# One trunk layer: RWKV products dealt to 64x64 tiles, gate projections spread over the four rounds, another order at the feed-forward entry

## The reference, cut to what matters

```
x = x + 0.5 * SwiGLU(RMSNorm(x))                 # feed-forward 1, D_FF = 2816
h = RMSNorm(x); P = h @ w_in                      # attention q,k,v | RWKV r,k,v,lora | 2 x 1024 gate columns
A = dilated window attention(P)                   # three groups
R = RWKV-7 time mixing(P)                         # 8 heads of 64, matrix state 64x64
x = x + w_out(sigmoid(gA) * (A @ w_branch_attn) + sigmoid(gR) * (R @ w_branch_rwkv))
x = x + 0.5 * SwiGLU(RMSNorm(x))                 # feed-forward 2

def step(S, r, w, k, v, kk, a):                   # RWKV-7, for each token in turn
    sk = S @ kk
    S = S * w - outer(sk, kk * a) + outer(v, k)
    return S, S @ r
```

## Time and profile before

| | before |
|---|---|
| median of three runs | 1737.68 us (1736.03 to 1738.81) |
| own time of the profiled execution | 1736.48 us |
| its span | 1734.6 us |
| PE busy | 1681.9 us, 97% of the span |
| DVE, ACT, POOL busy | 953.0, 737.8, 710.2 us (55, 43, 41%) |
| chain that ended last | PE 85%, DVE 9%, ACT 2% |
| fills and units, L396 | three passes, 1232 matmuls each |
| rounds 1, 2, 3 of RWKV begin | 552.11, 640.20, 729.22 us |
| next stage begins on PE | 803.67 us |

### The profile page before, as it was taken

The page is one execution under the profiler, slowest core; times in us unless marked ns, Lnnn a source line. Parts: engine busy times, 40 slices in busy tenths (PEclk is TensorE's granted clock), DMA queues, the critical chain, the costliest instruction groups (busy, mean ns, idle before and its releaser), DMA issues.

```text
span 1734.6 us, 41459 instructions
## 1 busy us (share of the span) xinstructions
PE 1681.9 (97%) x16564; PEld 1602.0 (92%) x16564; DVE 953.0 (55%) x1484; ACT 737.8 (43%) x1226; POOL 710.2 (41%) x912
## 2 busy tenths in 40 slices
PE   6899999999899999999999999999999899999999
PEld 6899999999799999998788989898999899999999
DVE  6836547366854545454475362727455945637363
ACT  5544536355523333332243443435334553536442
POOL 4554645555322222121132323324255573645643
PEclk9999999999899999999899999999999999999999
DMA  5353433423332334232055453446463352343512
GB/s 183 121 186 110 133 110 122 157 85 136 142 138 77 105 117 146 89 102 71 32 212 186 172 186 145 165 157 238 143 228 121 130 193 95 116 148 112 192 61 107
DMA packets 57497, 237.30 MB, mean 137 GB/s; under 512 B 7520, under 2 KB 8160, under 8 KB 55904
## 3 DMA queue, kind: packets, MB, share of 16 engines
q1 hardware_dynamic: 49440, 218.35, 35.7%
q10 hardware_dynamic: 7872, 16.37, 2.5%
HBM read 216.93 MB, written 71.76 MB: 166 GB/s over the span
## 4 chain that ended last, share of the span: by engine, by line
PE 85%; DVE 9%; ACT 2%; issue 1%; DVEq 1%; POOL 0%; DMA 0%; ACTq 0%
PE ps L396 29%; PE ps L825 23%; PE ps L835 16%; PE ps L1428 4%; PE ps L2375 1%; PE ps L2550 1%; PE ps L2475 1%; PE ps L2419 1%; PE ps L2497 1%; DVE T_lo L964 1%; PE ps L2459 1%; DVE B_lo L964 1%; PE ps L2490 0%; ACT w_hi L376 0%; DVE hf L1748 0%
## 5 line engine op out<-in xcount | busy, mean ns | idle before, releaser
L383 POOL TENSOR_TENSOR w_lo<-w_raw,w_hi 128x256 fp32r<-128x256 f32 x384 | 320.1, 864 | 685.4 <-ACT w_hi L376 685.4
L396 PE MATMUL ps<-h_hi,w_hi 128*128 128x288 f32 x1232 | 289.2, 316 | 19.5 <-POOL w_lo L383 13.9
L396 PE MATMUL ps<-h_hi,w_lo 128*128 128x288 f32 x1232 | 265.2, 297 | 0.0
L396 PE MATMUL ps<-h_lo,w_hi 128*128 128x288 f32 x1232 | 264.8, 297 | 0.0
L396 PEld LDWEIGHTS ps<-h_hi,w_hi 128*128 128x128 f32 x1232 | 200.1, 191 | 41.6 <-POOL w_lo L383 14.5
L396 PEld LDWEIGHTS ps<-h_lo,w_hi 128*128 128x128 f32 x1232 | 200.0, 190 | 0.0
L396 PEld LDWEIGHTS ps<-h_hi,w_lo 128*128 128x128 f32 x1232 | 199.5, 190 | 0.0
L808 POOL TENSOR_TENSOR ring_lo<-raw,ring_hi 128x256 fp32r<-128x256 f32 (+1 forms) x197 | 147.3, 772 | 112.3 <-ACT ring_hi L789 111.5
L376 ACT ACTIVATE w_hi<-w_raw 128x1024 fp32r<-128x1024 f32 x96 | 101.7, 1060 | 107.9 <-PE ps L396 93.6
L825 PE MATMUL ps<-T_hi,ring_hi 128*128 128x288 f32 x396 | 118.4, 299 | 11.1 <-ACT u L1052 8.7
L1235 DVE SCALAR_TENSOR_TENSOR x<-ps,x 128x576 f32<-128x576 f32 x64 | 48.5, 758 | 139.5 <-PE ps L835 138.2
(11 more groups left out here) (454 smaller groups left out, 3975.2 us busy)
## 6 DMA issues: line engine op xcount, KB each, us to landing
w_raw<-in_w SPq DMA_DIRECT2D x122, 512.0 KB, 3.4
raw<-in_w SPq DMA_DIRECT2D x48, 512.0 KB, 4.9
kv<-in_kc SPq DMA_DIRECT2D x32, 576.0 KB, 6.6
kv<-in_vc SPq DMA_DIRECT2D x32, 576.0 KB, 7.3
cache_out<-in_cache SPq DMA_DIRECT2D x28, 576.0 KB
raw<-in_w_down SPq DMA_DIRECT2D x32, 384.0 KB, 3.4
w_raw<-in_w_down SPq DMA_DIRECT2D x16, 384.0 KB, 3.7
gates<-gate_out ACTq DMA_DIRECT2D x16, 288.0 KB, 2.3
```

Source lines behind the costliest of these rows:

```text
L383: last = nc.gpsimd.tensor_tensor(w_lo[par_][:, c], w_raw[par_][:, c], w_hi[par_][:, c].bitcast(F32), ALU.subtract)
L396: last = nc.tensor.matmul(ps[:, b + c, 0:HC], w[par_][:, wk], a[:, k, c * HC:(c + 1) * HC], start=(first and k == 0), stop=(end and k == n ...
```

## The change

1. **Dealing of the fills.** `FILL` becomes a table for each round. The 200 slices are dealt 53, 48, 48, 51. The units between the mix units are three gate units a round, the last round has three more in place of the next round's mix units, and gate unit 15 is the last of all.
2. **ACT's order in the rounds.** `gate_out(ct - 1, 3)` and its early `split_hi` go. `gate_out(12)`, `(13)`, `(14)` stand in round 3 where other rounds have `take`; `gate_out(15)` stands behind the last evacuation, ahead of the barrier.
3. **Products by head.** `whole_product` deals its two heads in turn instead of one after the other. GG is computed for each head alone, 16 products of 64x64 instead of 8 of 128x128, of which half was thrown away; its tile shrinks, its evacuation becomes one DVE instruction instead of two, and the clearing of the tile at the start of the stage (a memset on DVE) goes. The state product of a chunk step becomes two of 64x64. The loops at L1544 and L1574 take the heads in turn; at L1574 PE waits for both heads' U before it starts.
4. **Feed-forward entry.** ACT takes block 4 and `chunk_u2` earlier, and `chunk_p2` and `chunk_u3` ahead of the blocks 9 and 10. DVE takes `chunk22` and `chunk11` of the first tiles earlier, between the blocks' low parts.

```diff
-FILL = {"norm": (1, 4, 4, 4), "tokens": (2, 3, 5, 2), "bonus": 1, "products": 2, "level": (5, 3, 3, 3, 3), "mv": 4, "xk": 3,
-        "chunk": (1, 1, 1, 1, 1, 1, 1, 1), "tail": (3, 2)}
+FILL_FIRST = {"norm": 1, "tokens": (2, 3, 5, 2), "bonus": 1, "products": 2, "level": (5, 3, 3, 3, 3), "mv": 4, "xk": 3,
...
+FILL_MID = {"norm": 3, "tokens": (2, 2, 3, 1), "bonus": 1, "products": 1, "level": (4, 3, 3, 3, 3), "mv": 3, "xk": 3,
...
+FILL_LAST = {"norm": 4, "tokens": (2, 2, 4, 1), "bonus": 1, "products": 2, "level": (4, 3, 3, 3, 3), "mv": 4, "xk": 3,
+             "chunk": (2, 1, 1, 1, 1, 1, 1, 1), "tail": (2, 1)}
+FILLS = (FILL_FIRST, FILL_MID, FILL_MID, FILL_LAST)
...
-    RW_UNITS += [("gate", _ct, n) for n in range(3)] + [("mix", _ct + 1, n) for n in range(3) if _ct + 1 < CT] + [("gate", _ct, 3)]
+    RW_UNITS += [("gate", 0, 3 * _ct + n) for n in range(3)]
+    RW_UNITS += [("mix", _ct + 1, n) if _ct + 1 < CT else ("gate", 0, 12 + n) for n in range(3)]
+RW_UNITS += [("gate", 0, 15)]
...
-            block_hi(act, f, 2)
-            block_hi(act, f, 3)
+            for i in range(2, 5):
+                block_hi(act, f, i)
             chunk_p2(n_cl)
-            for i in range(4, 7):
-                block_hi(act, f, i)
+            block_hi(act, f, 5)
+            block_hi(act, f, 6)
+            chunk_u2(n_cl)
             operand_hi(act, f, "T4")
-            chunk_u2(n_cl)
...
                 if i:
                     block_hi(act, f, i + 7)
+                if i == 1:
+                    chunk_p2(n_cl + 1)
+                    chunk_u3(n_cl)
...
+                if i == 1:
+                    chunk22(T0)
+                    block_lo_dve(dve, f, 8)
+                    made_s(dve, f, ("S1", T0 + 1))
+                elif i == 2:
+                    chunk11(T0 + 1)
+                    block_lo_dve(dve, f, 9)
+                    made_s(dve, f, ("S2", T0 + 1))
+                elif i != 3:
+                    behind(i)
...
+                    def whole_products(n, lhs, rhs):
+                        for h in range(2):
+                            bank_free(n, h)
                         for T in range(4):
...
+                            for h in range(2):
+                                last = nc.tensor.matmul(ps[:, 4 + (2 * n + h) % 4, T * 128:(T + 1) * 128], tile_of(lhs, T, h),
+                                                        tile_of(rhs, T, h), start=True, stop=True)
...
-                        for e in range(2):
-                            tok = slice(64 * e, 64 * e + 64)
-                            last = nc.tensor.matmul(ps[:, 5 + e, 128 * T:128 * T + 128], XTK[tok, T, :], TOK[tok, 1, T, :],
-                                                    start=True, stop=True)
+                        for h in range(2):
+                            for e in range(2):
+                                last = nc.tensor.matmul(ps[rows_of(h), 5 + e, 64 * T:64 * T + 64], XTK[rows_of(e), T, rows_of(h)],
+                                                        TOK[rows_of(e), 1, T, rows_of(h)], start=True, stop=True)
...
-                        nc.tensor.matmul(ps[:, IN_BANK[e], 64 * T:64 * T + 64], GG[:, e, T, :], ST[:, ch, :], start=False, stop=True,
-                                         skip_group_check=True).then_inc(sem("ds_done"), 1)
+                        for h in range(2):
+                            rows = rows_of(h)
+                            last = nc.tensor.matmul(ps[rows, IN_BANK[e], 64 * T:64 * T + 64], GG[rows, e, T, :], ST[rows, ch, :],
+                                                    start=False, stop=True, skip_group_check=True)
...
-                    for h in range(2):
-                        rows = rows_of(h)
-                        pe.wait_ge(sem("u_ready"), 2 * ct + h + 1)
-                        for T in range(4):
+                    pe.wait_ge(sem("u_ready"), 2 * ct + 2)
+                    for T in range(4):
+                        for h in range(2):
...
-                    if ct:
-                        P, q = rw_unit("gate", ct - 1, 3)
-                        split_hi(act, P + 1, q, W8)
...
-                    if ct:
-                        gate_out(ct - 1, 3, split_early=True)
...
                     else:
-                        gate_out(ct, 3)
+                        gate_out(12)
...
+            gate_out(15)
```

More of the change, by code:

```diff
@@ L1246, in ffn_dve @@
                     g_low(b[1] - 1)
-                behind(i)
-                if b[0] == "A11" and b[1] != first_tile(f, p):
+                if i == 1:
[8 more added lines that the diff above has]
+                    behind(i)
+                if b[0] == "A11" and b[1] not in (first_tile(f, p), T0 + 1):
                     chunk22(b[1] - 1)
@@ L1375, in rwkv_pe @@
                         last.then_inc(sem("lora_done"), 1)
-                    fill(FILL["norm"][ct])
+                    fill(FILL["norm"])
                     pe.wait_ge(sem("kk_sq"), ct + 1)
@@ L1478, in rwkv_pe @@
                             n += 2
-                    for lhs, rhs in ((KH, KA), (BH, RH), (KH, RH)):
-                        for h in range(2):
-                            bank_free(n, h)
-                            if lhs is KH and rhs is KA:
-                                product(n, h, of_chunk(lhs, h), of_chunk(rhs, h))
-                            else:
-                                whole_product(n, h, lhs, rhs)
-                        n += 1
+                    for h in range(2):
+                        bank_free(n, h)
+                        product(n, h, of_chunk(KH, h), of_chunk(KA, h))
+                    whole_products(n + 1, BH, RH)
+                    whole_products(n + 2, KH, RH)
+                    n += 3
                     assert n == NPROD
@@ L1674, in rwkv_act @@
                         act.drain()
-                    gate_out(ct, 1)
+                    gate_out(3 * ct + 1)
                     for lv in range(5):
@@ L1682, in rwkv_act @@
                         if lv == 2:
-                            gate_out(ct, 2)
+                            gate_out(3 * ct + 2)
                     if ct + 1 < CT:
@@ L1698, in rwkv_act @@
                         take("mix", ct + 1, 1)
+                    else:
+                        gate_out(13)
                     for half in range(2):
@@ L1706, in rwkv_act @@
                         take("mix", ct + 1, 2)
+                    else:
+                        gate_out(14)
                     act.wait_ge(sem("o_done"), ct + 1)
@@ L1861, in rwkv_dve @@
                     dve.wait_ge(sem("gg_done"), ct + 1)
-                    for h in range(2):
-                        rows = rows_of(h)
-                        ins = V.tensor_tensor(GG[rows, :, :, rows], ps[rows, 5:7, :].rearrange("p e (t n) -> p e t n", n=128)[:, :, :, rows],
-                                              K("id2")[rows].unsqueeze(1).unsqueeze(1).to_broadcast([64, 2, 4, DH]), ALU.add)
-                    ins.then_inc(sem("gg_evac"), 1)
+                    V.tensor_tensor(GG[:, :, :, :], ps[:, 5:7, 0:256].rearrange("p e (t n) -> p e t n", n=DH),
+                                    K("id2").unsqueeze(1).unsqueeze(1).to_broadcast([128, 2, 4, DH]), ALU.add).then_inc(sem("gg_evac"), 1)
                     dve.drain()
```

39 lines of the change are left out of this document (20 added, 19 removed).

## The result

| | before | after |
|---|---|---|
| median of 10 runs | 1737.39 us (1733.38 to 1745.12) | 1749.58 us (1742.41 to 1755.49) |
| ratio, 95% interval | | 1.0073 (1.0059 to 1.0087) |
| own time and span of the profiled execution | 1736.48, 1734.6 us | 1751.49, 1749.7 us |
| PE busy | 1681.9 us | 1680.1 us |

The change makes the kernel 12 us slower. Forecast were 1743 us and a range up to 1749; the direction was right, the size was not: +5.4 was the sum against the profiled execution, which shows +15.0. The runs of the changed kernel spread over 13 us, and their times follow the granted clock of the core: 1742.41 us at a mean of 0.994, 1755.49 at 0.984.

What follows compares the result with a forecast made beforehand. PE, busy 97% of the span, was taken as the bound. Terms -6.6 - 6.5 + 19.3 + 1.7 - 2.5 = +5.4 on 1736.48 gave 1741.9; with 1.2 for the median, 1743 us, range 1731 to 1749.

Steps and rivals of the forecast that it cites:

- one half-clock stretch of 1.7 us: Round 3: PE standing still 3.3 us for weights would bring one stretch at half clock, +1.7 us.
- POOL's four pieces: Weight split for the twelfth slice: POOL's part would take 3.4 to 3.7 us after ACT's split of 1.06.
- The terms of the products: Four rounds: GG 1.8 us less, output loops 3.9, state product 0.9; sum -6.6, bounds -10 and 0.
- feed-forward 1 entry: Copy wait gone, D at 92.9 instead of 96.19, 0.95 lost again at the next S3: -2.35 us.
- rounds 1 and 2: Eight slices fewer each, 6.3 us of PE work, of which waits leave 3.25 a round: -6.5 us together.
- The state product: Chunk step's L1538 in 64x64 saves a change of tile form: 0.03 us a step, 0.9 in 28 steps.
- The row that the forecast gave for it: L1428, 64 records in 1.56 us, taken as showing that two row halves overlap in one PSUM bank.
- The rival that gives the whole stall back: Both feed-forward entries lose their waits and half-clock stretches, 12.6 us in place of 2.5: 1733.0 us; chance 0.13.
- The wait at the twelfth slice: PE waits for POOL's weights where a new unit opens: 3.3 us in round 3, 0.8 in rounds 1 and 2.
- The waits at the twentieth and twenty-eighth slice: Round 3, levels 0 and 3: weights late by 2.4 us, of which 1.1 counts, and by 1.7.
- More half clock: Rival: waits in rounds 1 and 2 and level 0 of round 3 bring two or three stretches at 1.7: 1747 us; chance 0.12.
- a sign of being wrong: Round 3 growing by under 14 or over 22 us, or its waits for weights under 3 us in total.

Runs made afterwards that it cites:

- e8: Kernel before with only the products by head, old dealing and old feed-forward entry: 1737.10 us, ratio 1.0008.
- e5: e2's kernel with three of round 3's 35 slices moved behind the inversion: 1729.24 us, ratio 0.9961.
- e10: Kernel before with only three slices of round 3 moved behind the inversion: 1737.89 us, ratio 1.0005.
- e12: Full change with two DVE instructions beside POOL's split cut to 8 columns and the one between multiplied by 0: 1744.16 us, one run.
- e2: Kernel before with products by head and the new feed-forward entry, old dealing and old ACT order: 1734.22 us, ratio 0.9985.
- e1: Kernel before with only the new dealing and ACT's new order, old products and old feed-forward entry: 1760.31 us, ratio 1.0137.
- e4: Full change with slices dealt 53, 46, 46, 55 in place of 53, 48, 48, 51: 1742.38 us, ratio 1.0028.
- e9: e5 with two more slices taken off the tail of round 2, 37 in round 3 in place of 35: 1726.80 us, ratio 0.9939.
- e7: Kernel before with only the new order at the feed-forward entry: 1735.03 us, ratio 0.9995.
- e3: Full change with the split that the twelfth slice needs put back to its early place: 1741.97 us, ratio 1.0037.

## Why the prediction was right in its way and wrong in its size

The step that failed is the clock: the forecast put one half-clock stretch of 1.7 us into round 3, and the trace has four in rounds 1 to 3 and at the barrier that cost some 7.7. A smaller one is POOL's four pieces, put at 3.4 to 3.7 us and measured at 4.50 to 4.92. The terms of the products and of the feed-forward 1 entry came out near their numbers, the second in part by luck; rounds 1 and 2 kept less of their fewer slices than forecast.

**Products by head: right by the traces.** GG and the output product of round 1 after, which answer to the earlier trace rows:

```profile
611.52 0.69 PE L1541 MATMUL ps<-tok,qkv 64*64 64x64 f32 x32
...
630.02 1.09 PE L1599 MATMUL ps<-lraw,qkv 128*64 128x128 f32 x16
```

GG took 0.69, forecast 0.7; the output product 1.09, forecast 1.1. Round 1 got 1.86 us shorter by this part (1.37 from GG to the end of the chunk steps, 0.49 at the output product), forecast 1.65. The whole products saved 0.6 and L1524 gave it back, as the earlier trace rows let expect. The state product, put at 0.03 a step, saved 0.06: a step from fill to fill takes 1.36 us in place of 1.42, and the product's own row reads, after and before:

```profile
621.10 0.33 PE L1562 MATMUL ps<-qkv,gg 64*64 64x64 f32 x4
...
627.66 0.33 PE L1538 MATMUL ps<-qkv,gg 128*128 128x64 f32 x2
```

Four records in the time of two, with its two row halves in one PSUM bank, on different partitions. The rule of the Trainium skill (TensorEngine Tiling (Array Packing), Restrictions and Gotchas) that different row tiles cannot use one bank at once does not show here as a loss. The row that the forecast gave for it (64 records in 1.56 us) is of another kind, since there each bank gets one head's products, from one row half; L1502 with 32 records in 1.15 is of the right kind. That the gain of this part would reach the total was the error: e8 has it in the trace and not in the time, and only e5 against e10 shows it in the time.

**Feed-forward entries: right in the numbers, in part by luck.** The start of A22 and of D in feed-forward 1, which answer to the earlier trace rows:

```profile
83.44 0.40 PE L832 MATMUL ps<-T_hi,ring_hi 128*128 128x288 f32 x1 [1.08 <-ACT u L1059]
...
92.80 0.54 PE L842 MATMUL ps<-g_hi,ring_hi 128*128 128x288 f32 x2 [1.45 <-ACT sg L1065]
```

D was forecast at 92.9 and the next S3 at -2.35; they came at 92.80 and -2.3. The rival that gives the whole stall back is refuted: PE waits for the silu and for DVE's low parts instead. But the forecast's path to D was wrong. It had `chunk12` at 89.9 and then 2.97 us until g_lo. The trace has:

```profile
91.42 0.46 DVE L1239 TENSOR_TENSOR gt<-u,ps 128x288 f32<-128x288 f32 x1
...
92.36 0.39 ACT L1065 ACTIVATE sg<-ps 128x288 f32<-128x288 f32 x1
...
95.71 0.76 DVE L1124 TENSOR_TENSOR g_lo<-gt,g_hi 128x576 fp32r<-128x576 f32 x1 [0.73 <-ACT g_hi L981]
```

`chunk12` (L1239) came 1.5 later, and D waited for the silu 1.4 behind it and not for g_lo, which came after D. The two errors cancel. Up to round 0 the kernel won 1.35 more than forecast, in a trace in which a half-clock stretch of 3.4 us (450.4 on, before) is missing; nothing in the forecast had that.

**The wait at the twelfth slice: right in place, too small.** Forecast 3.3 in round 3 and 0.8 in rounds 1 and 2, measured 4.15 and 1.1. The step that failed here is "the split 1.06, then POOL's four pieces 3.4 to 3.7". The early split of the kernel before had 1.7 us of DVE's work with both inputs in SBUF beside it; at its new place it has 3.7 to 4.1, and POOL takes 4.50 to 4.92 us, while DVE's own instructions there go from 0.76 to between 1.10 and 1.17; e12 shows that the two are linked. In rounds 1 and 2 the fourth transpose, which waits for that slowed DVE chain, comes 1.0 late (L1808), forecast 0.4. The waits at the twentieth and twenty-eighth slice were forecast at 2.4 and 1.7; together with the first they make 7.9 in round 3, forecast 7.4.

**The clock: the term that was mis-sized, and the largest part of the miss.** I had put one half-clock stretch in round 3, 1.7 us, and one in feed-forward 2, 1.3. The trace has 16.7 us of them in rounds 1 to 3 and at the barrier, with PE busy for 15.3, so some 7.7 are lost: 6.0 more than the 1.7 of the forecast, of 9.6 us that it missed in all. Feed-forward 2 came to +1.3 up to D instead of -0.2. Its stretch of 6.8 us lies wholly in work; the kernel before also had 6.8 there (1385.6 to 1392.5), of which 2.5 passed in the wait. "More half clock", given 0.12, was the nearest rival. Round 3 comes out at +22.9 in place of +19.4 by this: 0.8 of longer wait and the rest clock. That is more than the 22 which the forecast had named as a sign of being wrong. Rounds 1 and 2 miss 4.1 together: 1.6 is clock, an idle time of 1.55 in round 2 without a releaser (687.65; before 0.73) is another part, and the longer waits are the rest; of the eight slices fewer, 6.3 us, they kept 0.6 and 1.3 and not 3.25. (The forecast's own terms for this add up to 3.0.)

**What nothing in the forecast had.** The parts are not additive. Dealing +23, products by head +1, feed-forward -1 make some +24 (with e2 for the last two, +20), the full change +12. The even dealing removes round 3's bare end, and with it the 20.5 us at half clock that the products by head bring there; in e8 that cost 5.3. The traces alone add up to within 2.7 us (e1 +20.5, e2 -2.7, full +15.1), and e1's is the fastest of its executions. The remaining gap is not explained. I had read the half clock of that end as a thing that the dealing takes away, but not asked what part 3 alone would do to it.

**Why dealing evenly costs.** The forecast's reason holds: with round 3's waits for weights gone (e4), 5 us of loss are left. Round 3 was only 2.95 us longer than its work, so a slice put there costs its full 0.79 us and more, and the slices taken from rounds 1 and 2 open holes at KA, BH and the inversion's first level.

## What to carry to other kernels

Where work is used as filling between the steps of a chain, deal it by the holes, not evenly: first ask of each place what a slice covers there and what it leaves open where it is taken, and move few slices. Set the place where a filling unit begins against the place where its weights are split, since the wait comes once for each unit and is larger than the gain of a slice. And judge a shortening of PE's work in a thin stretch by the clock as well, in the mean clock of all executions and not in one trace: with three slices moved there the traced execution had 6.8 us at half clock in place of 20.5, and a change that hardly gained (e2, 0.9985) gains 0.4 to 0.6% (e5, e9). Whether the slices did it, or the idle time in the inflow that went with the move, is open.

## What the runs showed of the hardware

- POOL's subtraction and DVE slow each other when DVE's instruction reads both its inputs from SBUF: POOL's four pieces take 2.78 to 2.83 us beside a DVE that is idle or takes an input from PSUM, 3.26 to 3.69 beside some instructions with both inputs in SBUF, 4.92 beside a dense chain of them; DVE's 576-column product goes from 0.76 to 1.1, its 256-column ones from 0.42 to between 0.60 and 0.94 (746.9 to 750.1 in the full change). The Trainium skill, GPSIMD Engine Reference, Key points, says that GpSimd shares its SBUF interfaces with VectorE and that VectorE's instructions with two SBUF inputs contend for them; e12 agrees, with 1.03 us for two such instructions cut short.
- The half-clock stretches are 3.4, 6.8, 13.7 or 20.5 us long and follow waits of PE or stand in thin parts. They differ between versions in places where these have the same code: at the new entry of feed-forward 2 there was 6.8 us of it in the full change and e4, 3.4 in e2, e7 and e9, none in e3 and e5, and the time up to D there moved by +1.3 to +1.4, about 0 and -1.4 to -1.5 with it. One execution's trace is a sample of these.
- PE can stand still for 0.7 to 1.75 us within short products without a releaser. In six traces with such an idle time, it ends 1.2 to 1.5 us after a 16 KB packet of queue q8, kind "instruction", has landed; its place moves with the code (round 2 in the kernel before, the full change, e1 and e12; round 3 in e2 and e8).
- 64x64 products that go round all four corners run at 0.02 us each (GG: 32 in 0.69), those that finish one row half before the other at 0.03 (U: 32 in 0.98). Two row halves wrote one PSUM bank on different partitions without a loss that shows (L1502: 32 in 1.15; the state product: 4 in 0.33).
